# S5 input powers made in rows from DRAM tables, chunk inputs as pairs of 64x64 tiles, lag kernels placed through DRAM

## The reference

```python
lam_bar = jnp.exp(lam * step)                                  # 64 groups x 64 states
b_bar = ((lam_bar - 1.0) / lam)[..., None] * lax.complex(b_re, b_im)   # 64 x 64 x 16
bu = jnp.einsum('gpc,btgc->btgp', b_bar, uf)
...
_, xs = lax.associative_scan(_lin_combine, (decay, bu), axis=1)
y = jnp.real(jnp.einsum('gcp,btgp->btgc', c, xs)) + d_skip * uf
```

## Time and profile before

| | us |
|---|---|
| median of 3 runs (1614.99 to 1617.03) | 1615.99 |
| profiled execution, its own time | 1616.37 |
| its span, first to last instruction | 1614.4 |
| PE busy | 1571.4 (97%) |
| PEld busy | 1546.4 (96%) |
| DVE busy | 1024.2 (63%) |
| ACT busy | 756.4 (47%) |
| POOL busy | 480.4 (30%) |

### The profile page before, as it was taken

How to read it: one execution, slowest core, us unless ns; L and a number is a source line. 1 busy time by engine, 2 the same in 40 slices (tenths; PEclk the granted TensorE clock), 3 DMA queues, 4 the chain that set the end, 5 groups by cost and what they waited for, 6 DMA issues and landing times.

```text
span 1614.4 us, 35306 instructions
## 1 busy us (share of the span) xinstructions
PE 1571.4 (97%) x12718; PEld 1546.4 (96%) x12718; DVE 1024.2 (63%) x1476; ACT 756.4 (47%) x1053; POOL 480.4 (30%) x620
## 2 busy tenths in 40 slices
PE   7899999999989999999999999999999999999997
PEld 6899999999979989999999999999999999999997
DVE  7454678778656657656676777777777764444441
ACT  6244345655556654444444544545454443333333
POOL 7992267677233420122111111211112110001100
PEclk9999999999999999999999999999999999999998
DMA  6786355554565567655555546454554565545451
GB/s 225 203 221 175 99 158 159 153 167 141 173 207 178 174 188 180 191 162 190 180 158 156 167 151 188 154 172 156 156 180 150 188 220 188 166 164 168 163 166 71
DMA packets 281750, 274.56 MB, mean 170 GB/s; under 512 B 23296, under 2 KB 278016, under 8 KB 280992
## 3 DMA queue, kind: packets, MB, share of 16 engines
q1 hardware_dynamic: 268752, 246.23, 50.2%
q10 hardware_dynamic: 11056, 19.90, 3.4%
q0 software_dynamic: 1856, 7.22, 1.3%
HBM read 260.83 MB, written 12.45 MB: 169 GB/s over the span
## 4 chain that ended last, share of the span: by engine, by line
PE 88%; ACT 5%; DMA 2%; DVE 2%; SPq 1%; issue 1%; ACTq 0%; POOL 0%; DVEq 0%; POOLq 0%
PE banks L439 28%; PE banks L441 28%; PE banks L440 28%; ACT tlag L740 2%; DMA raw<-in_w_in 1%; PE banks L447 1%; DVE wlo L981 1%; ACT whi L715 1%; PE banks L566 1%; ACT L817 1%; DMA scratch_mask<-wks 1%; SPq L314 1%; PE banks L621 0%; PE banks L588 0%; PE banks L634 0%
## 5 line engine op out<-in xcount | busy, mean ns | idle before, releaser
L981 DVE TENSOR_TENSOR wlo<-raw,whi 128x1024 fp32r<-128x1024 f32 x444 | 559.3, 1272 | 317.2 <-ACT whi L715 311.9
L715 ACT ACTIVATE whi<-raw 128x1024 fp32r<-128x1024 f32 x444 | 461.9, 1051 | 480.2 <-PE banks L441 401.8
L439 PE MATMUL banks<-h_hi,whi 128*128 128x288 f32 x1408 | 415.4, 295 | 2.0 <-DVE wlo L981 1.9
L441 PE MATMUL banks<-h_hi,wlo 128*128 128x288 f32 x1408 | 416.4, 296 | 0.0
L440 PE MATMUL banks<-h_lo,whi 128*128 128x288 f32 x1408 | 416.4, 296 | 0.0
L439 PE MATMUL banks<-hhi,whi 128*128 128x288 f32 (+1 forms) x912 | 275.3, 302 | 19.7 <-DVE wlo L981 16.0
L441 PE MATMUL banks<-hhi,wlo 128*128 128x288 f32 (+1 forms) x912 | 270.6, 297 | 0.0
L440 PE MATMUL banks<-hlo,whi 128*128 128x288 f32 (+1 forms) x912 | 270.5, 297 | 0.0
L439 PEld LDWEIGHTS banks<-h_hi,whi 128*128 128x128 f32 x1408 | 264.9, 188 | 2.5 <-DVE wlo L981 2.1
L440 PEld LDWEIGHTS banks<-h_lo,whi 128*128 128x128 f32 x1408 | 265.2, 188 | 0.1
L441 PEld LDWEIGHTS banks<-h_hi,wlo 128*128 128x128 f32 x1408 | 265.1, 188 | 0.0
(11 more groups left out here) (311 smaller groups left out, 2338.4 us busy)
## 6 DMA issues: line engine op xcount, KB each, us to landing
raw<-in_w_up SPq DMA_DIRECT2D x352, 256.0 KB, 3.4
raw<-in_w_in SPq DMA_DIRECT2D x224, 256.0 KB, 3.3
raw<-in_w_down SPq DMA_DIRECT2D x176, 256.0 KB, 2.8
raw<-in_w_glu SPq DMA_DIRECT2D x64, 256.0 KB, 2.9
raw<-in_w_out SPq DMA_DIRECT2D x64, 256.0 KB, 3.2
raw<-in_w_attn_proj SPq DMA_DIRECT2D x32, 256.0 KB, 4.3
scratch_gates<-gt ACTq DMA_DIRECT2D x16, 288.0 KB, 3.0
xt<-in_x_t ACTq DMA_DIRECT2D x4, 576.0 KB, 7.2
```

Source lines behind the costliest of these rows:

```text
L439: pe.matmul(out, h, xh[:, kt, :], start=kt == 0, stop=False)
L441: mm = pe.matmul(out, lo, xh[:, kt, :], start=False, stop=kt == nk - 1)
L715: act.activation(whi[:, s, :, 0:cols], raw[:, s, :, 0:cols], ACT.Copy).then_inc(hi_ready, 1)
L981: dve.tensor_tensor(wlo[:, s, :, 0:cols], raw[:, s, :, 0:cols], whi[:, s, :, 0:cols], ALU.subtract).then_inc(lo_ready, 1)
```

## The change

1. **Input powers.** POOL no longer spreads all input powers into `blam` for PE to transpose. It makes, once before the stage, `flam_rows` (two copies); PE transposes these once (two transposes, `powers_t()`), ACT copies them to `ft` and writes them to DRAM (`flam_t`, 2 transfers). From there each turn's table `lt` comes back in two broadcast transfers (`powers_in`); a table of B (`bt`, 256 KB for a turn, made on the host as `s5_b2`) comes with one. `input_powers` is now four products and two full-partition combinations straight into `lbs`. The `powers_t` and `powers` of every turn go.
2. **Chunk inputs** are 16 matmuls of 64x64 instead of 8 of 128x128, in pairs on opposite corners; `ub` is laid out by half, channel and lag, and `steps_in` issues two transfers each time.
3. **Newest inputs.** What the lag kernels need of `blam` (lag 0 alone) is made by POOL's new `newest_inputs`: four products of 128x64 and four combinations of 64x64.
4. **Lag kernels.** ACT copies the result once (`tk`, 128x128); SP writes it to DRAM with four transfers (128 rows of 128 bytes each) and reads it back, shifted for each lag, with two (`lags_out`, `lags_in`). The 16 copies go.
5. **Order.** `tab` has two buffers, so `tables` no longer waits for the turn's `xs_ready`; its last operation is moved behind the evacuation (`decays`). In POOL's turn `input_powers(it + 1)` now waits for `bu_ready`, because `lbs` is a single buffer, and runs before `newest_inputs`, `output_powers` and `turn_forward`. SP's loop over the turns is written out.

```diff
+            def tables_in(it):
+                sp.wait_ge(sem("lbs_ready"), 2 * it - 2)
+                sp.dma_start(bt[it % 2]..., I["s5_b2"][:, 512 * it:512 * it + 512]).then_inc(sem(f"bt_in{it % 2}"), 16)
+                powers_in(sp, it)
+            def lags_out(it):
+                sp.wait_ge(sem("tk_ready"), it + 1)
+                if it:
+                    sp.wait_ge(sem("tlag_in"), 32 * it)
+                for i in range(4):
+                    sp.dma_start(W["lag"][:, LC - 1:, i, :], tk[32 * i:32 * i + 32, :]...).then_inc(sem("lag_out"), 16)
+            def lags_in(it):
+                sp.wait_ge(sem("lag_out"), 64 * it + 64)
+                if it:
+                    sp.wait_ge(sem("y_ready"), it)
+                ...
+                for n in range(2):
+                    sp.dma_start(tlag[64 * n:64 * n + 64, :, :, :]..., shifted).then_inc(sem("tlag_in"), 16)
+            for it in range(N_GATE):
+                for q in range(8):
+                    load("w_in", ...)
+                    if q == 2 and it < N_GATE - 2:
+                        tables_in(it + 2)
+                    if q == 4:
+                        lags_out(it)
+                    if q == 7:
+                        lags_in(it)
...
             def chunk_inputs(it):
...
-                        mm = pe.matmul(aux[:, c, NCH * i:NCH * (i + 1)], lbs[:, i, c, :], ub[:, it, i, :], start=True, stop=True)
+                        for n in range(2):
+                            r = slice(NST * n, NST * (n + 1))
+                            mm = pe.matmul(aux[r, c, NCH * i:NCH * (i + 1)], lbs[r, i, c, :], ub[r, it, i, :], start=True, stop=True)
...
-                group(0, 7 + it, c + 4, KD, hhi, hlo, before={0: (lambda: powers_t(it + 1, 0),), 1: (lambda: powers_t(it + 1, 1),),
-                                                              2: (lambda: lag_kernels(it + 1),)} if more else {})
+                group(0, 7 + it, c + 4, KD, hhi, hlo, before={2: (lambda: lag_kernels(it + 1),)} if more else {})
...
-                for k in range(LC):
-                    for i in range(4):
-                        ins = act.activation(tlag[it % 2][32 * k:32 * k + 32, i, 32 * (LC - 1 - k):P], aux[32 * i:32 * i + 32, 2, T:T + 32 * (k + 1)], ACT.Copy)
-                ins.then_inc(sem("tlag_ready"), 1)
+                act.activation(tk[:, :], aux[:, 2, T:T + P], ACT.Copy).then_inc(sem("tk_ready"), 1)
...
+            for k in range(2):
+                act.dma_start(bt[k]..., I["s5_b2"][:, 512 * k:512 * k + 512]).then_inc(sem(f"bt_in{k}"), 16)
             act.wait_ge(sem("ms_ready"), 1)
...
-                act.dma_start(ub[:, 2 * k:2 * k + 2, :, :], W["steps"][k].rearrange("b h m i a -> (b h) m i a")).then_inc(sem("ub_in"), 16)
+                for n in range(2):
+                    act.dma_start(ub[64 * n:64 * n + 64, ...], W["steps"][k][:, 16 * n:16 * n + 16]...).then_inc(sem("ub_in"), 16)
...
             hi_q(C_Q + 8, 0)
-            powers(0, 0)
+            act.wait_ge(sem("flam_t"), 1)
+            act.activation(ft[:, :, :], aux[:, 3, 0:2 * P]..., ACT.Copy).then_inc(sem("ft_ready"), 1)
             hi_q(C_Q + 8, 1)
-            powers(0, 1)
+            act.wait_ge(sem("ft_ready"), 1)
+            for n in range(2):
+                act.dma_start(W["flam_t"][n]..., ft[:, :, NST * n:NST * (n + 1)]).then_inc(sem("lam_out"), 16)
             hi_q(C_Q + 8, 2)
             lags(0)
+            act.wait_ge(sem("lam_out"), 32)
+            for t in range(2):
+                powers_in(act, t)
             hi_q(C_Q + 8, 3)
...
             for it in range(N_GATE):
+                if it < N_GATE - 1:
+                    input_powers(it + 1)
                 if 0 < it < N_GATE - 1:
-                    input_powers(it + 1)
+                    newest_inputs(it + 1)
                     output_powers(it + 1)
                 turn_forward(it)
```

More of the change, by code:

```diff
@@ L202, in hybrid_decoder_step_kernel @@
     xb = at("xb", [P, 2, 4, NCH], F32, WK + 16128)
-    tab = at("tab", [P, 2, 4, NCH], F32, WK + 18432)
+    tab = [at(f"tab{i}", [P, 2, 4, NCH], F32, (GR + 5120, WK + 18432)[i]) for i in range(2)]
     rm = at("rm", [P, 4, NCH], F32, WK + 20736)
@@ L567, in s5_outputs @@
                             else:
-                                mm = pe.matmul(out, tlag[jt % 2][:, i, 32 * b:32 * b + 32], ub[:, jt, i, :], start=False, stop=True)
+                                mm = pe.matmul(out, tlag[:, b, i, :], ub[:, jt, i, :], start=False, stop=True)
                 mm.then_inc(sem("y_ready"), 1)
@@ L723, in hi_q @@
                 ins.then_inc(hi_ready, 1)
[L725 to L730, removed]
             def lags(it):
                 act.wait_ge(sem("lag_t"), it + 1)
-                act.wait_ge(sem("tlag_clear"), 1)
-                if it > 1:
-                    act.wait_ge(sem("y_ready"), it - 1)
-                for k in range(LC):
-                    for i in range(4):
-                        ins = act.activation(tlag[it % 2][32 * k:32 * k + 32, i, 32 * (LC - 1 - k):P], aux[32 * i:32 * i + 32, 2, T:T + 32 * (k + 1)], ACT.Copy)
-                ins.then_inc(sem("tlag_ready"), 1)
+                if it:
+                    act.wait_ge(sem("lag_out"), 64 * it)
+                act.activation(tk[:, :], aux[:, 2, T:T + P], ACT.Copy).then_inc(sem("tk_ready"), 1)
             act.dma_start(nvec[:, :], I["norm_vecs"]).then_inc(sem("nv_in"), 16)
@@ L1209, in sample_index @@
                 dve.wait_ge(sem("scs_ready"), 1)
-                own(dve.memset(tab[:, 0, :, NCP:NCH], 1.0))
-                own.link(dve.memset(tab[:, 1, :, NCP:NCH], 0.0))
+                for t in tab:
+                    own(dve.memset(t[:, 0, :, NCP:NCH], 1.0))
+                    own(dve.memset(t[:, 1, :, NCP:NCH], 0.0))
+                own.wait()
             dve.wait_ge(sem("tok_stored"), 16 * 3)
@@ L1515, in _ @@
                 tt(flam[:, c, :, 1:LC], b1, b2, op)
+            for c in range(2):
+                copy(
+                    flam_rows[:, :, :, :, c], flam[:, c, :, :].rearrange("p (t i) k -> p t k i", i=4)).then_inc(sem("flam_ready"), 1)
             pool.wait_ge(sem("st_in"), 16)
@@ L1547, in output_powers @@
                     pool.wait_ge(sem("y_ready"), it - 1)
-                products(it, lam, 1, cnat)
+                products(it, lam, LC, cnat)
                 for n in range(2):
@@ L1560, in _ @@
             pool.wait_ge(sem("bn_in"), 16)
-            for it in range(2):
-                input_powers(it)
-                output_powers(it)
+            newest_inputs(0)
+            output_powers(0)
+            input_powers(0)
+            newest_inputs(1)
+            output_powers(1)
             for b in range(2):
@@ L1690 @@
 }
-_SCRATCH = {"x_kept": (P, KD * T), "wi": (4, IH, DS, 2), "gates": (32, P, T), "mask": (TS, SK), "v_new": (TS, KV), "steps": (4, LC, 32, 2, 4, NCH)}
+_SCRATCH = {"x_kept": (P, KD * T), "wi": (4, IH, DS, 2), "gates": (32, P, T), "mask": (TS, SK), "v_new": (TS, KV), "flam_t": (2, 2 * P, NST), "lag": (32, 2 * LC - 1, 4, 32), "steps": (4, LC, 32, 2, 4, NCH)}
 def build(nc, shapes):
```

112 lines of the change are left out of this document (73 added, 39 removed).

## The result

The changed kernel takes 1626.5 us (median of 4 runs, 1624.96 to 1627.96), the kernel before beside it 1616.2: a ratio of 1.0064, 95% interval 1.0047 to 1.0082. It is slower by 0.6%; I had forecast 1601 and a range up to 1611. The profiled execution has a span of 1625.1 us.

The account below looks back on a forecast made before the run. The prediction took PE's weight-chunk matmuls, 84% of the span, as the bound. Its terms, -5.2 - 6.2 - 0.6 - 2.4 - 0.6 = -15.0 us, gave 1601.4, as a median 1601.0, range 1597 to 1611.

Parts of the forecast that it names:

- POOL's, which I costed at 0: POOL's longer row of steps in each gates turn: `clam` ready at 21.6 us, wanted by PE at 22.4; cost 0.
- hits: DVE instructions holding up POOL before `clam`: five subtractions at 0.96 and six short operations at 0.4, 7.3 us in all.
- A margin of 0.8 us: Gap in a gates turn between `clam` ready at 21.6 us and PE wanting it at 22.4; taken to hold.
- the rival that POOL is late: PE waits at `lag_kernels` for `clam`, 1.3 us in six turns: 1609 us, range 1604.5 to 1614; chance 0.27.
- The turn's end: PE's stall for DVE's `lo` behind ACT's lag-kernel copies goes: 7 x 0.74 = -5.2 us.
- Chunk inputs: 32 records on 64x64 tiles at each turn's start take 1.4 us instead of 1.7: 8 x -0.3 = -2.4 us.
- the rival without overlap: 64x64 chunk-input matmuls don't run concurrently: inputs take 3.6 us, 1619 us in all, slower; chance 0.05.
- The transposes: PE transposes dropped, two a turn in seven turns at 0.44: -6.2 us; before the stage eight become two: -0.6.
- The index scores' wait: PE's 1.00 us wait for ACT's `rel` ahead of the stage shrinks: -0.6 us, ends -1.0 and +1.5.
- the start: Two 256 KB `bt` loads issued by ACT early in the kernel might hold up a weight chunk: 0, upper end +2.
- SP's longer turns: Nine more SP issues a turn, about 4.5 us, and three waits, ahead of later chunks' weight loads: cost 0.
- the transfers: Rival: transfers with 128-byte rows delay the weight chunks behind them; gain eaten when landings pass 8 us; chance 0.04.

Follow-up runs that it names:

- inplace: Changed kernel with lam combinations written over `bt`, input powers run one turn earlier behind `turn_forward`, and SP's `tables_in` waiting for `bu_ready`; 1598.4 us, ratio 0.9889.
- turn0: Changed kernel with only the input powers of turn 1 moved behind turn 0's turned output powers; 1624.2 us, ratio 1.0044.
- before_lagdma: Kernel before the change, with only the lag kernels going by one ACT copy and transfers through DRAM instead of sixteen copies; 1609.0 us, ratio 0.9948.
- tables_wait: Changed kernel with DVE's decay tables of the next turn also waiting until POOL has finished this turn's lam combinations; 1610.4 us, ratio 0.9961.
- keeper: Changed kernel with 20 unread matmuls added ahead of PE's wait in `lag_kernels`, from turn 2 on; 1619.5 us, ratio 1.0013.

## Why the prediction was wrong

**The step that failed is POOL's, which I costed at 0.** I had `clam` ready at 21.6 us against 22.4 wanted. The second number is right (PE stood from 22.4 on); the first was 25.1, 12.7 of own work and 11 of hits in place of 7.3. Three groups carry 10.5 of these 11: input products 5.10 us where 2.4 are free of DVE, newest products 3.82 where I had 1.0, the last combinations 7.97 where inplace shows 2.94. I had priced a hit as one DVE instruction each, from rows of 2.40 for 1.44 and of 1.33 for 0.59 on average, and had written that the two engines take turns. In the traces one POOL instruction waits through several DVE instructions that follow without a gap: 3.43 us for 0.74. The Trainium skill (SBUF — State Buffer, Who interferes with whom) has the shared port as an exclusive lock in which the other side blocks fully. The lengths agree, and they show that the one who waits need not get the next turn.

**A margin of 0.8 us in a sum of 20 was no ground for 0.** Its neighbour, the rival that POOL is late, was named with its place and its turns, but sized wrongly twice: the stall was 2.9 us and not 1.3 to 2.5, and I gave no price to the clock behind it, 1.5 us in five of six turns. 6 x 2.9 + 5 x 1.5 = 25 us where I allowed 15. Even that 15 was not carried through: with it the time would have been 1616, above the 1614 at which I ended this rival and the 1611 at which I ended the range.

**What POOL does to DVE was missing.** I costed the hits in one direction. In turn 0 DVE's tables took 2.2 us more beside the moved input powers, and PE waited 2.8 for `lo`, with half clock behind: 3.0 us, which turn0 takes away.

**The rest of the sum held in total, in part by luck.** The turn's end gave 0.76 us (0.74 forecast; before_lagdma). Chunk inputs 0.55 a turn (0.3), since 32 records of 64x64 go in 1.15 us: the rival without overlap is refuted. The transposes are the remainder of a turn's 2.08: 0.77 (0.88). The index scores' wait gave 0.74 (0.6), but the start cost 1.7 (0), so the changed kernel enters the stage level and inplace 0.5 us early, where I had 1.2. SP's longer turns and the transfers show in no wait of the stage. In inplace, where POOL is out of the way, PE is 14.9 us ahead at the stage's end; my sum was 15.0. That they agree is luck: the chunk inputs gave 2.0 us more in all than I had, against 0.8 less from the transposes, 0.7 less ahead of the stage, and a stall of 0.7 for `lo` in turn 0 that I had not.

**Not in my account at all:** the 3.7 us near 790, of a wait on DVE put down to issue and what follows on PE. A like step, 3.5 us at this place, is why inplace ends at 1598.4, below my 1601. Open is by what rule such a place costs; and whether turn 5's clock stayed up for a reason, since its wait was as long as the others'.

## What to carry to other kernels

When work moves onto an engine that is three quarters busy, count what it is late for, not how busy it is: POOL had the same 28 us of work in the version 28 us faster. A step whose slack is smaller than the uncertainty of its sum gets a price, and the price of a stall of PE includes the half clock that may follow it. Put POOL's two-input work where DVE has gaps, and don't compare kernels at the level of 0.2% without looking for waits put down to issue.

## What the hardware showed that I had not expected

- One POOL instruction of 0.74 us took 3.43 while DVE's subtraction and four table products passed it at their usual 1.20 and, a pair, 0.74; with the tables held back it took 2.09. In turn 0 it was DVE that paid, 1.46 and 1.83 us for a pair that takes 0.76.
- Waits of PE of 2.8 to 2.9 us had half clock behind them in most cases but not in all (not in turn 5 of the changed kernel, nor in turn 0 of tables_wait and keeper), and one of 2.67 hadn't; each fall cost about 1.5 us. Filled with matmuls nobody reads, the wait had none behind it in six turns.
- 34, 26 or a loop of 32 added matmuls in one place changed waits at other places, up to 860 us later, from 0.5 to 8.5 us in sum.
